# A two-block transformer kernel on one core: the first layer's modulation in four quarters, with the q and part of the k projection between them, and table angles made by GpSimd

## The reference, cut to what matters

```
silu_c, silu_cc = silu(c), silu(c_ctx)
shift, scale, gate       = split(silu_c  @ w_mod[l] + b_mod[l], 3)    # 2048 -> 3 * 2048
shift_c, scale_c, gate_c = split(silu_cc @ w_mod[l] + b_mod[l], 3)
n  = rms_norm(h,  pre_norm_g[l]) * (1 + scale)   + shift              # 256 rows
nc = rms_norm(hc, pre_norm_g[l]) * (1 + scale_c) + shift_c            # 256 rows
p, pc = split(n @ w_in[l]), split(nc @ w_in[l])                       # 13 parts: q, k, v, ... gate
```

## Time and profile before

| what | value |
|---|---|
| median of 3 runs | 3254.26 us (3253.12 to 3257.14) |
| the profiled execution: time, span | 3250.3 us, 3248.5 us |
| PE busy | 2958.3 us (91%) |
| DVE busy | 1950.4 us (60%) |
| ACT busy | 1118.0 us (34%) |
| POOL busy | 247.4 us (8%) |
| granted TensorE clock, mean | 0.944 |
| HBM read, written | 459.07 MB, 13.11 MB |

### The profile page before, as it was taken

How to read it: one execution, slowest core, us unless ns; L and a number is a source line. 1 busy time by engine, 2 the same in 40 slices (tenths; PEclk the granted TensorE clock), 3 DMA queues, 4 the chain that set the end, 5 groups by cost and what they waited for, 6 DMA issues and landing times.

```text
span 3248.5 us, 40339 instructions
## 1 busy us (share of the span) xinstructions
PE 2958.3 (91%) x15557; PEld 2384.8 (73%) x15557; DVE 1950.4 (60%) x3426; ACT 1118.0 (34%) x1788; POOL 247.4 (8%) x269
## 2 busy tenths in 40 slices
PE   6889889999899979989998978878989999999998
PEld 1177567788678867767876767754688999999887
DVE  5377877676767754454253547777355666666444
ACT  2142322333223234333332433222343444444443
POOL 0000000000000000000001004545000000000000
PEclk9999899999999989999998988987698999999999
DMA  8855244454434533232332443321033555555555
GB/s 307 289 181 172 72 133 143 149 176 131 147 130 179 186 135 118 78 110 91 114 114 77 156 145 109 117 94 51 27 130 127 185 183 182 182 183 186 200 191 168
DMA packets 149808, 474.82 MB, mean 146 GB/s; under 512 B 16864, under 2 KB 17888, under 8 KB 148448
## 3 DMA queue, kind: packets, MB, share of 16 engines
q1 hardware_dynamic: 137664, 431.03, 40.2%
q10 hardware_dynamic: 9392, 32.30, 2.7%
q0 software_dynamic: 2560, 8.91, 0.9%
HBM read 459.07 MB, written 13.11 MB: 145 GB/s over the span
## 4 chain that ended last, share of the span: by engine, by line
PE 53%; issue 29%; DVE 9%; DMA 3%; POOL 2%; ACT 2%; ACTq 0%; DVEq 0%; POOLq 0%
PE bank L915 15%; PE bank L916 14%; PE bank L917 14%; DMA common<-w_mod 2%; PE bank L932 2%; PE bank L1097 1%; DVE split_weights L1226 1%; POOL common L2288 1%; PE bank L1019 1%; PE bank L1160 1%; PE bank L1112 1%; ACT split_weights L1885 1%; POOL first_block_work L2313 1%; PE bank L1000 1%; PE bank L1104 1%
## 5 line engine op out<-in xcount | busy, mean ns | idle before, releaser
L1226 DVE TENSOR_TENSOR split_weights<-common,split_weights 128x1024 fp32r<-128x1024 f32 x628 | 779.4, 1249 | 746.7 <-ACT split_weights L1885 680.6
L1885 ACT ACTIVATE split_weights<-common 128x1024 fp32r<-128x1024 f32 x628 | 656.6, 1053 | 1052.0 <-PE bank L917 986.9
L915 PE MATMUL bank<-split_weights,features 128*128 128x512 f32 x1920 | 803.6, 419 | 7.9 <-DVE features L1370 3.4
L917 PE MATMUL bank<-split_weights,features 128*128 128x512 f32 x1920 | 757.7, 395 | 0.0
L916 PE MATMUL bank<-split_weights,features 128*128 128x512 f32 x1920 | 757.3, 394 | 0.0
L915 PEld LDWEIGHTS bank<-split_weights,features 128*128 128x128 f32 x1920 | 366.5, 191 | 107.9 <-issue 30.9
L916 PEld LDWEIGHTS bank<-split_weights,features 128*128 128x128 f32 x1920 | 367.0, 191 | 77.9 <-issue 11.5
L917 PEld LDWEIGHTS bank<-split_weights,features 128*128 128x128 f32 x1920 | 365.7, 190 | 79.3
L915 PE MATMUL bank<-ffn_input_split,split_weights 128*128 128x256 f32 (+1 forms) x1376 | 392.9, 286 | 2.8 <-DVE ffn_input_split L1650 1.8
L916 PE MATMUL bank<-ffn_input_split,split_weights 128*128 128x256 f32 (+1 forms) x1376 | 391.5, 284 | 0.0
L917 PE MATMUL bank<-ffn_input_split,split_weights 128*128 128x256 f32 (+1 forms) x1376 | 391.1, 284 | 0.0
(11 more groups left out here) (279 smaller groups left out, 3336.0 us busy)
## 6 DMA issues: line engine op xcount, KB each, us to landing
common<-w_in SPq DMA_DIRECT2D x252, 512.0 KB, 3.3
common<-w_up SPq DMA_DIRECT2D x172, 512.0 KB, 4.2
first_block_work<-w_mod_cols SPq DMA_DIRECT2D x256, 256.0 KB, 3.7
common<-w_out SPq DMA_DIRECT2D x96, 512.0 KB, 3.3
common<-w_down SPq DMA_DIRECT2D x84, 512.0 KB, 3.3
common<-w_mod SPq DMA_DIRECT2D x64, 512.0 KB, 4.9
trig<-common ACTq DMA_DIRECT2D x32, 272.0 KB, 5.0
second_block_work<-trig POOLq DMA_DIRECT2D x32, 272.0 KB, 3.4
```

Of the source, the lines that this page charges most:

```text
L915: e.matmul(out_ap, xs[0], ws[0], start=first, stop=False)
L917: return e.matmul(out_ap, xs[0], ws[1], start=False, stop=last)
L1226: e.tensor_tensor(lo, raw, hi.bitcast(F32), ALU.subtract).then_inc(*low_done.tick(("lo", m)))
L1885: e.activation(split_slots[:, 0, i, 0:words], raw_slots[:, m % RAW, 0:words], ACT.Copy).then_inc(*high_done.tick(("high", m)))
```

## The change: what it does

1. The weight plan has the q and k pieces of layer 0 first, two of q and two of k in turn. `w_mod` leaves the plan: its 64 pieces come by `mod_load_first` into eight slots of their own, which lie where the old stream was; `x` and `ctx` are loaded to another place.
2. The eight chunks are taken as (0, 4), (1, 5), (2, 6), (3, 7): a quarter of shift, then the same quarter of scale. After each quarter its four feature tiles are made. Two banks hold the sums, one for shift and one for scale.
3. The transposes of the normalised rows come before scale and shift: after chunk 0 all 64 run at once (`x_turn`), with copies to SBUF by ACT and DVE.
4. During quarters 1 to 3, behind every fourth modulation piece, stands one piece of products for the features of the quarter before: two pieces of q (four row tiles), two of k (the two `x` tiles). The last four come after the loop. The k projection of the two `ctx` tiles is a normal `project` after that and loads k's eight pieces again.
5. Table angles are made by POOL, into one of two buffers, one table per two modulation pieces; the last ones and `tables_end` stand between the loop and the last four pieces.
6. `self.background.append(self.modulation())` stays behind the first stage, which now holds all of q and half of k.

```diff
-    plan = [A["w_mod"][c, g] for c in range(MOD_FIRST) for g in range(KT // KP)]
+    plan = [A["w_in"][0, c, g] for first in range(0, KT // KP, 2) for c in IN_ORDER[:2] for g in (first, first + 1)]
     for l in range(DEPTH):
-        for c in IN_ORDER:
+        for c in IN_ORDER[0 if l else 1:]:
...
+    def first_stage(self):
...
+        for _ in range(MOD_SLOTS):
+            self.mod_load()
+        pieces = []
+        for i in range(4):
+            late = None
+            for c in (i, 4 + i):
+                for kg in range(KT // KP):
+                    self.do("mod_products", c, kg, done)
+                    done += 1
+                    self.mod_load()
+                    if late is not None and kg == 1:
+                        self.do("mod_turn", late)
+                        late = None
+                    if i or c:
+                        step += 1
+                        if step % 2:
+                            self.do("table_angles", step // 2)
+                            if step > 2:
+                                self.do("table", step // 2 - 1)
+                    if kg % 4 == 3 and pieces:
+                        self.first_products(*pieces.pop(0))
+                late = c
+                if c == 0:
+                    for f in range(KT):
+                        self.do("x_turn", f)
+                    self.weights()
+            self.do("mod_turn", late)
+            self.do("mod_scale", 0, i)
+            for f in range(4 * i, 4 * i + 4):
+                self.do("normed_first", f)
+                if f % 4:
+                    self.do("normed_first_split", f - 1)
+            self.do("normed_first_split", 4 * i + 3)
+            pieces = [(p, tiles, bank, kg) for p, tiles, bank in ((q, range(NT), 0), (k, range(LT), NT))
+                      for kg in (2 * i, 2 * i + 1)]
+        for j in range(step // 2, SJ):
+            self.do("table", j - 1)
+            self.do("table_angles", j)
+        self.do("table", SJ - 1)
+        self.do("tables_end")
+        for piece in pieces:
+            self.first_products(*piece)
...
+    def first_products(self, p, tiles, bank, kg):
+        finish = self.heads(0, 0, "diff", "q" if bank == 0 else "k", HEADS)
+        m = self.take()
+        for t in tiles:
+            for k in range(KP):
+                self.do("products", self.feature_set, p, t, bank + t, kg, k, m, t == tiles[-1] and k == KP - 1)
+                self.side()
+            if kg == KT // KP - 1:
+                finish(p, t, bank + t)
+            self.side()
...
+                if l == 0 and g == 0 and part in "qk":
+                    if part == "k":
+                        self.project(tiles[LT:], self.heads(l, g, kind, "k", HEADS))
...
+        def table_angles(j):                      # GpSimd
+            x = trig_x[j % 2]
+            for s, n in seen.new(at("steps"), at("coefficients", "ci"), at("table_made", j - 2) if j > 1 else START):
+                e.wait_ge(s, n)
+            for s_ in range(2):
+                e.tensor_scalar(x[:, s_, :], steps_row, ssm_ph[:, j:j + 1], 0.25 * (1 - s_), ALU.mult, ALU.add)...
+            e.tensor_scalar(trig_w, x, HALF_UP, -HALF_UP, ALU.add, ALU.add)...
+            e.tensor_tensor(x, x, trig_w, ALU.subtract)...
...
+        def mod_load_first(w):                    # SyncE
+            for s, n in seen.new(at("mod_used", w - MOD_SLOTS) if w >= MOD_SLOTS else START):
+                e.wait_ge(s, n)
+            e.dma_start(mod_slots[:, w % MOD_SLOTS, :], A["w_mod"][MOD_ORDER[w // (KT // KP)], w % (KT // KP)])...
```

More of the change, by code:

```diff
@@ L315, in whole @@
         self.do("steps")
[L316 to L329, removed]
+        self.first_stage()
         self.background.append(self.modulation())
@@ L340, in whole @@
         return self.steps
+    def first_stage(self):
+        self.feature_set = ("normed", 0)
+        self.turn += 1
+        step, self.mod_loaded, done = 0, 0, 0
+        q, k = self.projections, self.projections + 1
+        self.projections += 2
+        for _ in range(MOD_SLOTS):
[40 more added lines that the diff above has]
+            self.first_products(*piece)
@@ L794, in build @@
     ssm.update(r=ssm_r, ph=ssm_ph, cr=ssm_cr, ci=ssm_ci)
-    steps_row, trig_x, trig_w = B.one(T2), B.two(2, T2), B.two(2, T2)
+    steps_row, trig_x, trig_w = rows_buf[1][:, 0:T2], [B.two(2, T2) for _ in range(2)], B.two(2, T2)
     trig_out = [B.two(2, T2) for _ in range(2)]
@@ L943, in mod_turn, with x_turn @@
             done.then_inc(*modulation_turned.tick(*names))
+        def x_turn(f):
+            tb = banks[f % 6]
+            for s, n in seen.new(tb.claim("x_turn", f)):
+                e.wait_ge(s, n)
+            for t in range(NT):
+                for s, n in seen.new(at("scaled", 0, t)):
+                    e.wait_ge(s, n)
+                done = e.transpose(tb[:, t * P:(t + 1) * P], hid[:, t, f * P:(f + 1) * P], ident)
+            done.then_inc(*features_turned.tick(("x_turned", f)))
         def normed_turn(l, f, x):
@@ L1934, in silu_row, with x_turn, normed_first, normed_first_split @@
                 *tables_made.tick(("silu_row_tanh", row, stream)))
+        def x_turn(f):
+            if f % 2 == 0:
+                return
+            for s, n in seen.new(at("x_turned", f)):
+                e.wait_ge(s, n)
+            e.activation(x_turned[:, f, :], banks[f % 6][:, :], ACT.Copy).then_inc(
+                *features_high.tick(("x_kept", f), ("free", "x_turn", f)))
+        def normed_first(f):
+            if f % 2 == 0:
+                return
+            for s, n in seen.new(at("x_kept", f), at("scales_ready", 0, f // 4), at("mod_added", 0, f // 4),
+                                 at("feature", "normed", 0, f - 2) if f > 1 else START):
+                e.wait_ge(s, n)
+            for s_ in range(2):
+                part = slice(s_ * LAT, (s_ + 1) * LAT)
+                e.activation(turn_b[:, part], x_turned[:, f, part], ACT.Identity, scale=scaled_g[0][:, f, s_:s_ + 1],
+                             bias=mod_all[0][:, f, s_:s_ + 1]).then_inc(*features_high.tick(*[("modulated", 0, f)] * s_))
+        def normed_first_split(f):
+            for s, n in seen.new(at("modulated", 0, f), at("scaled", 0, NT - 1)):
+                e.wait_ge(s, n)
+            e.activation(feat[:, 0, f, :], (turn_a, turn_b)[f % 2], ACT.Copy).then_inc(
+                *features_high.tick(("feature_high", "normed", 0, f)))
         def normed_turn(l, f, x):
@@ L2393, in build @@
     raw_loaded = [loading(f"raw{i}_loaded") for i in range(RAW)]
+    first_loaded = [loading(f"first{i}_loaded") for i in range(MOD_SLOTS)]
     mod_loaded = [loading(f"mod{i}_loaded") for i in range(MODRING)]
```

159 lines of the change are left out of this document (102 added, 57 removed).

## The result

| kernel | median, us | against before, 95% interval |
|---|---|---|
| before, 20 runs | 3254.66 | |
| after, 20 runs | 3259.55 | 1.0014 (1.0008 to 1.0020) |

The change costs 4.9 us: clear of zero, but under the 0.2% (6.5 us) that the prediction took as its mark. The forecast was 3261.5. The profiled execution of after took 3259.14 us with a span of 3257.2, 8.7 us over the profiled span of before.

What follows compares the result with a forecast made beforehand. PE was taken as the bound, busy 91%, with room where it waits for w_mod loads in the first stage. Terms -10.8 + 15 + 3 = +7.2 on 3250.3 give 3257.5, median 3261.5; range 3240 to 3284.

Steps and rivals of the forecast that it cites:

- the sum: Whole kernel: -10.8 us by k's end, +15 at layer 0's end, +3 in the gate projections, +7.2 on 3250.3.
- The loop: First stage up to the last modulation and between-product work: PE's terms from a 12.5 us start add to 197.3 us.
- E: The time at which the modulation loop ends, 197.3 us; beyond 205 or under 190 would make the prediction wrong.
- PE's wait for the rows: Behind chunk 0, PE waits for ctx, whose load shares the queues with five more w_mod pieces: 3.3 us (0 to 6).
- The tail: Behind the loop: last features, Sins, three tables of 4.0 us and the last store, 23.5 us (19 to 32).
- After the tail: Splits, heads, last q and k pieces, then k for ctx: 46.9 us, k ending at 267.7, gain 10.8.
- The steps left over: At layer 0's end, before row_scale: 14 missing background steps, 13 of them pieces, run on DVE, costing 15 us (11 to 20).
- The gate projections: Attention groups 3 and 4 of layer 0: background 24 steps later, 12 us more DVE each, mostly hidden, +3 (0 to 8).
- POOL did not bound the changed kernel's loop: Rival: POOL is the bound, a table at 7 us or more, +34 us, 3296; chance 0.08.
- DMA did not bound the loop: Rival: DMA bounds the loop as tables collide with loads, +2 us in each of four chunks and at the start, 3271; chance 0.10.
- The faster rival: PE's list has no gaps up to the loop's end, 9.3 us off; at best -9.1, median 3245; chance 0.20.
- The slow start after a wait: Matmuls after waits start at the slow pace: 1.5 us in the loop and 1.5 us behind the tail.

Runs made afterwards that it cites:

- run 6: The changed kernel with three slots for w_mod instead of eight: 3267.55 us, 8.0 above the changed kernel, 1.0043 against before.
- run 4: The changed kernel with POOL's rounding as two multiply-add tensor-scalars instead of one with two additions: 3259.54 us in one run.
- Run 1: The changed kernel with the 14 missing background steps taken in the first 14 pieces of layer 0's output projection: 3248.27 us, 0.9984 against before.
- run 3: The changed kernel with 14 background steps taken earlier and all tables spread inside the loop, angles still on POOL: 3246.05 us, 0.9975 against before.
- run 8: The changed kernel with angles on VectorE, all tables spread over the loop, 14 background steps taken one in every seventh piece: 3240.48 us, 0.9960 against before.
- run 9: Run 8's kernel with only three tables in quarter 0, the rest behind the first splits: 3231.45 us, 0.9934 against before.
- runs 1 to 4: The changed kernel with background steps earlier, with tables inside the loop, with both, with POOL's rounding split: 3248.27, 3255.86, 3246.05, 3259.54 us.
- run 10: Run 9's kernel with the fourth to eighth w_mod pieces held back until constants or x have landed: 3231.07 us, 0.9930 against before.

## Why the prediction was right

The sign, the size and the two places were as forecast. The likeliest class was not: slower by more than 0.2% had 0.54, and what came is within it, which had 0.24. Luck has a part in how close 3259.55 is to 3261.5: behind the gap at layer 0's end the two traces differ by 11.1 us where the sum had 7.2. What took it back is no part of the argument: 2.4 us in layer 1, where before's execution had the lower clock, and 4.0 since before's execution lay 4.4 us below its median and after's only 0.4. Point by point:

- **The loop.** E, with the last turn, was forecast at 197.3; the turn's transposes are in the chain at 198.3. Three terms were off and two of them cancelled. The first matmul came at 14.65, not 12.5, past the bound of 14: the last constants took 6.5 us to land instead of 3.8, and with three slots (run 6) the first matmul is at 11.76. But PE's wait for the rows was the shorter for it (1.0, forecast 3.3), so the transposes began at 32.29 (32.6 forecast). The first product waited 4.1 us (3.0).
- **The tail.** 4.5 us for a table against 4.0, three times: 222.1 for the last store against E + 23.5 = 220.8. The dear term inside was not where I looked: the multiply-adds with a column as the factor took 0.48 us each, the tensor-tensor 1.34, the rounding 2.03. PE's hole, 16.6 us, is the forecast's tail and first head together (E + 11.8 to E + 30.2 would be 18.4); the text named only 12 of it, up to the tail's end, and its sign to look for, a hole that ends about 220, was 9 us early.

The Trainium skill, GPSIMD Engine Reference, section 4.1, puts one-input operations near line rate. For the multiply-add run 4 agrees roughly (0.65 us for 544 columns, against 1.34 for two inputs); for the form with two additions the trace of after does not (2.03 us), and the measurement decides.

- **After the tail.** k was done, and v's first product came, at 268.7 (before: 278.4), forecast 267.7; -9.6 against -10.8. Run 1, the same list up to here, has 267.4, so such times scatter by a microsecond or so.
- **The steps left over.** 16.9 us; forecast 15, with 11 and 20 as ends. The prediction counted thirteen pieces, the trace has fourteen; one more at its own 1.27 would have made the forecast 16.3. The ring sets it: ten of them waited for their load, 5.4 us in all. Run 1 takes fourteen steps earlier, and the gap is gone.
- **The gate projections.** 3.8 lost between 279 and 1066 us, forecast 3; the number is right and the place for the most part wrong. The forecast had it in the gate projections of groups 3 and 4; the trace has 0.8 in group 3's (DVE had the 12 us more to do there) and none in group 4's, but 1.0 in group 1's and 2.0 at the start of the output projection. No run took this term alone.
- **The rivals.** POOL did not bound the changed kernel's loop (last product at 195.2), and cost 6 us at its end once the list asked for more (run 3 against run 8). DMA did not bound the loop: PE waited there for no load, and run 6 gives the price of less depth, 8 us. The faster rival asked for a PE list without gaps: the gaps were there.
- **The slow start after a wait.** The sum has it twice, at 1.5 us. The chain shows nine matmuls of 0.43 us instead of 0.23 after the wait at 65.7, which is 9 x 0.2 = 1.8, and as long a slow stretch after the hole at 229. There are two more that no part named, behind the waits of 3.1 and 2.6 us (eight matmuls from 203.7, six from 245.0). The granted clock is 0.50 at 66 to 70 and at 229 to 233 us, and 0.53 at 244.4 to 248. After 1.9 us of wait (run 9) it stayed at 1.00.

What stays open is the 4 us between the medians and the traces. The executions of before that ran beside runs 1 to 4 had a mean granted clock of 0.944 (three, median 3251.6 us), 0.943 (seven, 3252.8), 0.942 (thirteen, 3255.2) or 0.941 (four, 3256.2). The profiled execution of before is one of the first kind (3250.3 us at 0.944); where the usual ones lose their time, no trace shows.

## What to carry to other kernels

Before work is moved ahead of a point where a background job starts, count the job's steps against its deadline: here 24 turns were lost, and what was owed ran at the layer's end, where nothing hid it, for 17 us, more than the 9.6 that the overlap won. Work that is moved "between" other work has a tail; look for what stands behind the loop in each engine's list (features, three tables and a store, 23 us), and for what an in-order engine must do ahead of the first step that another engine waits for. An engine that is nearly idle is not by that the better place: GpSimd's 4.5 us a table stood where PE waited for them, three in a row; on the busier VectorE a table took 1.9. With the background's debt spread thin, the tables' angles on VectorE and only three tables ahead of the first split, the same change is 0.66% faster than before instead of 0.14% slower.

## What the runs showed of the hardware

- GpSimd, tensor-scalar, 544 float32 columns: 2.03 us for add then add with constants, 0.65 us for multiply then add with constants. 272 columns with a column as the factor: 0.48 us. Tensor-tensor, 544: 1.34 us alone, 1.43 in the mean.
- VectorE for the same: 0.446 (544, add and add), 0.356 (272), 0.727 (tensor-tensor). A table is 1.9 us there and 4.5 on GpSimd.
- Eight loads of 512 KB queued at the start delay a 448 KB load on another queue (6.5 us to landing; with three, 3.6 in run 6 and 3.8 before): the first matmul behind it came at 14.6 to 16.0 us in the runs with eight, at 11.76 with three; `ctx` landed at 26.1 instead of 21.1. Holding loads back brought nothing (run 10).
- A ring of three 256 KB loads, each issued when the slot is free, gave one piece per 1.23 us once the first three were used up (from 1198.30 to 1210.57 us for ten), where VectorE alone needs 0.90 from start to start.
- In after, TensorE's granted clock was 0.50 to 0.53 for some 4 us behind each of the waits of 4.1, 16.6 and 2.6 us (0.43 us a matmul of 512 columns instead of 0.23). Behind 1.9 us of wait in run 9 it was 1.00.
